# Two blocks on one core: merged rows made in columns, maxima before the gates' sums, compressed values made in columns, other places for the first query pieces

## The reference

```
blocks = t[:, :, tok] + pos
return blocks.reshape(B, G, n_cmp, CMP_LEN * dh) @ w
```

```
def merge(m, a, gates):
    g_m, g_a = jnp.split(gates, 2, axis=-1)
    return (jax.nn.sigmoid(g_m) * (m @ w_bm) + jax.nn.sigmoid(g_a) * (a @ w_ba)) @ w_out
```

## Time and profile before

| What | us |
|---|---|
| Median of the runs | 1293.1 |
| Profiled execution, its own time | 1294.55 |
| Span of that execution, first to last instruction | 1292.4 |
| TensorE busy with products | 1159.1 |
| VectorE busy | 860.6 |
| ScalarE busy | 313.9 |
| GpSimd busy | 326.1 |
| Mean granted TensorE clock, as a share of full speed | 0.981 |
| Memory traffic in all | 391.23 MB, mean 303 GB/s |

### The profile page before, as it was taken

The page is one execution under the profiler, slowest core; times in us unless marked ns, Lnnn a source line. Parts: engine busy times, 40 slices in busy tenths (PEclk is TensorE's granted clock), DMA queues, the critical chain, the costliest instruction groups (busy, mean ns, idle before and its releaser), DMA issues.

```text
span 1292.4 us, 14563 instructions
## 1 busy us (share of the span) xinstructions
PE 1159.1 (90%) x5048; PEld 695.6 (54%) x5048; DVE 860.6 (67%) x2306; ACT 313.9 (24%) x1008; POOL 326.1 (25%) x285
## 2 busy tenths in 40 slices
PE   8999999999999989999999889889877877778777
PEld 5876668867855677864566445445322322223332
DVE  2747745275545767873688777777778777777655
ACT  0115300234211122330232222222222222222222
POOL 0000000000001000000244454455554454554440
PEclk9999899999999999999999999999999899999999
DMA  8861155842343557632899999999999999999994
GB/s 340 308 253 66 65 195 210 301 156 99 125 195 134 213 160 267 244 130 98 318 405 424 424 424 424 425 424 424 423 424 422 424 424 424 423 421 424 423 424 200
DMA packets 54824, 391.23 MB, mean 303 GB/s; under 512 B 8120, under 2 KB 10680, under 8 KB 15840
## 3 DMA queue, kind: packets, MB, share of 16 engines
q0 software_dynamic: 37792, 269.63, 50.4%
q1 hardware_dynamic: 16960, 120.68, 24.9%
HBM read 389.22 MB, written 1.07 MB: 302 GB/s over the span
## 4 chain that ended last, share of the span: by engine, by line
PE 54%; DMA 34%; DVE 9%; ACT 2%; issue 1%; POOL 0%; SPq 0%; DVEq 0%; ACTq 0%
PE bank L541 20%; DMA wring<-peer_uv_in,arena 15%; PE bank L547 13%; PE bank L1124 10%; DMA const<-peer_uv_in,arena 7%; DMA arena<-peer_uv_in,arena 6%; DMA hT<-peer_uv_in,arena 5%; PE bank L576 2%; DVE arena L1601 1%; PE bank L769 1%; DVE arena L1609 1%; PE bank L613 1%; PE bank L599 1%; PE bank L683 1%; PE bank L741 1%
## 5 line engine op out<-in xcount | busy, mean ns | idle before, releaser
L1124 PE MATMUL bank<-arena 128*128 128x512 f32 x460 | 221.4, 618 | 44.0 <-ACT arena L1568 43.5
L1124 PE MATMUL bank<-wring,arena 128*128 128x512 f32 x340 | 164.2, 619 | 38.0 <-ACT arena L1568 38.0
L547 PE MATMUL bank<-hT,wring 128*128 128x256 f32 (+1 forms) x1088 | 188.9, 333 | 0.8 <-ACT arena L1346 0.8
L547 PEld LDWEIGHTS bank<-hT,wring 128*128 128x128 f32 x1088 | 169.2, 192 | 26.5 <-issue 11.2
L2317 DVE CUSTOM_DVE_ANT_0 arena<-arena 128x1024 f32<-128x1024 f32 x115 | 140.4, 1223 | 55.4 <-DMA arena<-peer_uv_in,arena 53.5
L1124 PEld LDWEIGHTS bank<-arena 128*128 128x128 f32 x460 | 85.8, 196 | 162.6 <-issue 93.0
L2422 POOL DMA_INDIRECT arena<-peer_uv_in,arena x114 | 131.8, 1156 | 162.5 <-PE bank L1124 136.3
L2387 POOL TENSOR_TENSOR small<-small,const 128x1 f32<-128x1 f32 (+3 forms) x18 | 16.7, 926 | 585.5 <-DVEq L1613 264.3
L541 PE MATMUL bank<-wring,hT 128*128 128x256 f32 (+2 forms) x544 | 157.9, 447 | 0.6 <-DVE arena L1601 0.6
L2317 DVE CUSTOM_DVE_ANT_0 wring<-wring,arena 128x1024 f32<-128x1024 f32 x85 | 103.9, 1223 | 44.1 <-DMA wring<-peer_uv_in,arena 43.2
L1124 PEld LDWEIGHTS bank<-wring,arena 128*128 128x128 f32 x340 | 63.2, 195 | 128.4 <-issue 65.5
(11 more groups left out here) (237 smaller groups left out, 1278.1 us busy)
## 6 DMA issues: line engine op xcount, KB each, us to landing
wring<-w_in SPq DMA_DIRECT2D x22, 2048.0 KB, 9.8
wring<-ada_in SPq DMA_DIRECT2D x12, 2048.0 KB, 8.4
wring<-wo_in SPq DMA_DIRECT2D x5, 2048.0 KB, 8.1
wring<-cmp_in SPq DMA_DIRECT2D x2, 2048.0 KB, 8.2
wring<-br_in SPq DMA_DIRECT2D x2, 2048.0 KB, 8.5
arena<-pq_in SPq DMA_DIRECT2D x2, 2048.0 KB, 9.4
wring<-pq_in SPq DMA_DIRECT2D x2, 2048.0 KB, 8.2
wring<-w1b_in SPq DMA_DIRECT2D x2, 1120.0 KB, 7.5
```

The lines of the kernel that those rows point to most:

```text
L547: ins = pe.matmul(bank[:, at:at + n_tok], w[:, k, col:col + P], rhs[:, k, :], start=(k == 0), stop=(k == KC - 1))
L1124: ins = pe.matmul(sums_of[half][:, :], diag[:, at % NDIAG, :], v_row[slot_of[at]][:, half * 512:(half + 1) * 512], start=(n == 0), stop=(n ...
```

## The change

**Compressed values.** The products get the keys' form: weights stationary, 15 columns moving, one bank `vcT` for both groups. ScalarE copies it to a corner of `cmp_s`, TensorE transposes it once behind the rotated queries and keys, and ScalarE copies the result to `vc` there.

**Maxima.** On VectorE `attn_max(0)` stands ahead of the running sums, `attn_scale(0)` behind them and ahead of the differences, `attn_max(1)` behind those, and the bias last.

**Merge.** `branch_gate` uses `project_t`, `branch` takes 16 products of 128 columns with the weights stationary, four side by side in a bank, and VectorE merges into `mrgT` directly, four blocks of 128. The transpositions of merged rows and their copies are gone; `out_rows` of half 0 waits for the first sum ahead of its first product and for the second ahead of the fifth.

**First rows.** The pieces of `plan` up to row 49 stand behind other rows, and the steps of heads 1 and 2 in `choice_at` too.

```
-        plan = [(row, ("q", 1, n, 0)) for n, row in enumerate((1, 1, 3, 3))] + [(5, ("ps", 0, 1)), (9, ("pT", 1))]
-        plan += [(row, ("q", 2, n, 0)) for n, row in enumerate((7, 11, 15, 19))] + [(21, ("ps", 0, 2))]
-        plan += [(row, ("q", 0, n, 1)) for n, row in enumerate((13, 17, 23, 25))]
-        plan += [(row, ("q", 3, n, 0)) for n, row in enumerate((31, 35, 39, 43))] + [(47, ("ps", 0, 3))]
+        plan = [(row, ("q", 1, n, 0)) for n, row in enumerate((1, 3, 5, 7))] + [(9, ("ps", 0, 1)), (11, ("pT", 1))]
+        plan += [(row, ("q", 2, n, 0)) for n, row in enumerate((13, 17, 21, 25))] + [(29, ("ps", 0, 2))]
+        plan += [(row, ("q", 0, n, 1)) for n, row in enumerate((15, 19, 23, 27))]
+        plan += [(row, ("q", 3, n, 0)) for n, row in enumerate((35, 39, 43, 47))] + [(49, ("ps", 0, 3))]
...
-            choice_at.setdefault(3 + n // 2, []).append((1, n))
+            choice_at.setdefault(3 + n * 5 // 16, []).append((1, n))
         for h in range(2, TT * EH):
-            first_row = 11 if h == 2 else 8 + 14 * (h - 2) if h < 6 else 16 * (h - 2)
+            first_row = 12 if h == 2 else 8 + 14 * (h - 2) if h < 6 else 16 * (h - 2)
             for n in range(16):
-                choice_at.setdefault(first_row + n * (11 if h == 2 else 14 if h < 6 else 16) // 16, []).append((h, n))
+                choice_at.setdefault(first_row + n * (10 if h == 2 else 14 if h < 6 else 16) // 16, []).append((h, n))
...
-                vc_bank = [job(("vc", L, g)) for g in range(2)]
+                bank = job(("vcT", L))
                 for l in range(CMP_L):
                     for g in range(2):
                         r = slice(g * HD, (g + 1) * HD)
-                        ins = pe.matmul(vc_bank[g][0:CMP_N, 0:HD], blocksT[r, 1, l, :], w[r, 1, l, :],
+                        ins = pe.matmul(bank[r, 0:CMP_N], w[r, 1, l, :], blocksT[r, 1, l, :],
                                         start=(l == 0), stop=(l == CMP_L - 1))
...
+                taken(pe, ("vcT", L))
+                bank = job(("vc", L))
+                finish(pe.transpose(bank[0:CMP_N, 0:P], vcT, ident), ("vc", L))
                 taken(pe, ("kc", L))
...
-                c, t, q = n // 4, (n // 2) % 2, n % 2
+                c, q = n // 4, n % 4
                 w = weights(("w2", 0, 6 + c)).rearrange("p (k c) -> p k c", k=KC)
-                project(("gate", n), [hlT[:, k, t * P:(t + 1) * P] for k in range(KC)], w[:, :, q * S:(q + 1) * S], S)
+                finish(project_t(job(("gate", n)), 0, w, q * P, hlT, S), ("gate", n))
...
-                project((name, half, t), [src[:, k, t * P:(t + 1) * P] for k in range(4)], wb[:, k0:k0 + 4, :], 512)
+                bank = job((name, half, t))
+                for q in range(4):
+                    for k in range(4):
+                        ins = pe.matmul(bank[:, q * P:(q + 1) * P], wb[:, k0 + k, q * P:(q + 1) * P], src[:, k, t * P:(t + 1) * P],
+                                        start=(k == 0), stop=(k == 3))
...
             def out_rows(half, t):
                 w = weights(("wo2", 0, half)).rearrange("p (k c) -> p k c", k=KC)
-                project(("wo2", half, t), [mrgT[:, k, t * P:(t + 1) * P] for k in range(KC)], w, 512)
+                bank = job(("wo2", half, t))
+                for k in range(KC):
+                    if half == 0 and k % 4 == 0:
+                        pe.wait_ge(sem("mrg"), 2 * t + k // 4 + 1)
+                    ins = pe.matmul(bank[:, :], mrgT[:, k, t * P:(t + 1) * P], w[:, k, :], start=(k == 0), stop=(k == KC - 1))
...
-            merged_transposes(0, 0)
             latent_transposes(1)
-            merged_transposes(0, 1)
...
-            merged_transposes(1, 0)
-            merged_transposes(1, 1)
             rows_back(0)
...
-            link(dve.memset(rows[7], 0.0))
...
             attn_max(0)
+            link(dve.memset(rows[7], 0.0))
...
+            attn_scale(0)
+            link(tt(rows[5], rows[0], rows[3], ALU.subtract))
+            link(tt(rows[6], rows[0], rows[4], ALU.subtract), "gate_rows")
             attn_max(1)
-            attn_scale(0)
+            add_bias(5, 6)
```

More of the change, by code:

```diff
@@ L1106, in _ @@
             head_scores(0)
-            merged_transposes(1, 0)
-            merged_transposes(1, 1)
             rows_back(0)
-            for half in range(2):
-                taken(pe, ("gT", 1, half))
             out_rows(0, 1)
@@ L1329, in _ @@
                     free(copy(retT[:, :, t * P:(t + 1) * P], bank[:, :].rearrange("p (j s) -> p j s", j=4)), ("rT", L, t))
+                bank = full(act, ("vc", L))
+                free(copy(vc[0:CMP_N, :], bank[0:CMP_N, 0:P]), ("vc", L))
                 for t in range(TT):
@@ L1500, in latent @@
                 free(copy(mT[:, :, t * P:(t + 1) * P], bank[:, :].rearrange("p (j s) -> p j s", j=4)), ("mT", t))
-            def merged(t):
-                for half in range(2 if t else 1):
-                    bank = full(act, ("gT", t, half))
-                    free(copy(mrgT[:, 4 * half:4 * half + 4, t * P:(t + 1) * P],
-                              bank[:, :].rearrange("p (j s) -> p j s", j=4)), ("gT", t, half))
             def x1_squares(t):
@@ L1544, in _ @@
             latent(0)
-            merged(0)
             latent(1)
```

53 lines of the change are left out of this document (22 added, 31 removed).

## The result

The changed kernel takes 1298.87 us (median of 6 runs, 1297.79 to 1300.24), the kernel before 1293.91 (6 runs): ratio 1.004, interval 1.0031 to 1.005. Slower by 0.4%, where 0.7% faster was forecast. The profiled execution has a span of 1296.0, 3.6 more than before.

A forecast was written before the change was run, and what follows sets the result against it. TensorE work, with VectorE pieces, bounds the kernel up to the first gather, expert-weight loads after it. 2.7 + 2.9 + 1.8 = 7.4, plus 0.5 and 1.0, gives 8.9 us off the median 1293.1: 1284.2, bounds 1281.5 to 1287.

The forecast's parts named there:

- Compressed values: Compressed stage of both layers: turned products save 1.47 less 0.13 for a transposition, 1.34 per layer, 2.7 us in all.
- Maxima: VectorE's order before the attention transpositions: TensorE's 2.86 us stop for scaled scores goes, worth 2.9 us, bounds 2.0 to 2.9.
- pause without a releaser: First layer's compressed stage: a pause that may go, counted only in the upper bound of 3.3 us.
- Gates, branches, merge: Before the first gather: gates nothing, merge saves 2.8, branches in columns lose 1.0; net 1.8 us, bounds 1.0 and 2.5.
- Behind the first gather: Second half of the kernel: 0.5 from earlier output projections and 1.0 from sparser first rows, 1.5 us together.
- gathers 2 to 8: First hole in the loads: their slots come 0.87 earlier without the merge's last transpositions; taken as 0.5 us, bounds 0 and 0.9.
- Head 1's indices: Selection on VectorE: done by row 7 instead of row 10, near 661, so gather 16 waits for its slot only.
- The second hole: Loads at 349 GB/s for 8 us from gather 16, 1.4 us lost; mostly goes, 1.0 us won, at worst 2 lost.
- (b): Rival: an early cut is taken up by a transfer or VectorE; 1287.1 if the maxima's 2.9 goes; chance 0.06.
- (d): Rival: the change doesn't do what it says, the transposed form's other waits cost what it saves: 1293; chance 0.03.

The follow-up runs named there:

- e8: The changed kernel with the gates' bias back in front of the maxima and compressed values in the old form: 1284.35 us, ratio 0.9944 to the kernel before.
- e1: The kernel before with the compressed values in columns alone: 1300.65 us, ratio 1.0057.
- e9: The changed kernel with the gates' bias early and every compressed key and value product moving 64 columns instead of 15: 1282.61 us, ratio 0.9921 to the kernel before.
- e13: The kernel before with only its compressed keys' products widened from 15 to 64 moving columns: 1290.34 us, ratio 0.9973.
- e5: The changed kernel with the bias of the gates' columns put back in front of the attention maxima: 1292.12 us, ratio 0.9995 to the kernel before.
- e14: The changed kernel, bias left late, with its thin compressed products widened to 64 moving columns: 1291.81 us, ratio 0.9984 to the kernel before.
- e2: The kernel before with the attention maxima in front of the gates' sums alone, the bias late: 1298.26 us, ratio 1.004.
- e11: The kernel before with the attention maxima first and the gates' bias kept early, nothing else: 1287.38 us, ratio 0.9955.
- e3: The kernel before with gates, branches and merge in columns alone: 1290.48 us, ratio 0.9973.
- e4: The kernel before with the sparser first rows and the denser selection alone: 1292.46 us, ratio 0.9994.
- e12: The changed kernel with bias early, compressed values in the old form and the row and selection tables of before: 1284.5 us, ratio 0.9933 to the kernel before.
- e6: The changed kernel with the compressed values' products in front of the keys': 1300.92 us, ratio 1.0063 to the kernel before.
- e10: The changed kernel, bias early, compressed keys and values both in the old form with 64 moving columns, keys then transposed: 1281.05 us, ratio 0.9914 to the kernel before.

## Why the prediction was wrong

**Compressed values: the step failed.** I took -1.34 per layer from two neighbouring rows, 5.31 us for the old form and 3.84 for the turned one, as the prices of two forms. They were taken at two clocks. At the full clock the old form takes 3.75 (e8) and the turned one 3.91, so the change had nothing to gain there but what the fall of the clock had cost. The one price that it did have stood in none of my terms: around the end of the keys' 15-column products the clock falls, and the turned form puts a second run of them there. They ran at the lower level, and so did part of the dense product behind them: +2.9 and +3.3 in the trace, 7 us for the step alone (e1). The two rows had a different granted clock, 1.00 and 0.68; the windows of that stretch would have shown it before any argument about forms. I also had the hint of a "pause without a releaser" in layer 0 and took its end for a possible gain; pauses of 0.43 and 0.36 us stand in e9 and e13 too, at a clock of 1.00, so they are not the fall.

By the rule of the Trainium skill (TensorE: Matmul & The Clock Gate, LDWEIGHTS) I had estimated 6.8 us for the turned form, and the trace now says 6.9. That is not the rule coming true: at the full clock the same 128 loads of 64 columns, with their products, take 3.8 to 4.1 us (3.91 for the keys in this trace, 3.95 in e9). The same page of the Trainium skill, in its section HAM oscillation — how this bites in real kernels, tells of a kernel with thin matmuls that falls back to the lower clock, in its case through waits for transfers. The trace shows the lower clock here without any wait for a transfer, behind the thin products themselves. So that part would not have forecast this loss as it stands, but it was the one about the clock, and I weighed the other one.

**Maxima: the gain was right, what is queued behind it was missed.** The stop of 2.86 went (-2.95) and with it 1.7 of lower clock that I could have read from the timeline of the kernel before: 8.75 for the second half against 7.17 for the first. The failed sentence is "SP waits for the gates' rows only together with a transposition that TensorE makes after its second half". It is true of the semaphore `gate_rows`. But SyncE's block waits for the bias as well, a few lines above, and the change puts the bias behind the second round of maxima. I had costed its end (462.1; it came at 469.2, which is 462.9 less the shift of 6.3) and not followed who waits for it: SyncE, a transfer of 10.9 us for 4 KB, and a heap of loads behind it. That was +6.4 in the trace, and 6 to 11 us between kernels with and without it (e5, e14, and e2 against e11).

**Gates, branches, merge: right.** 1.8 forecast, 1.8 in the trace; 3.4 us with what it frees (e3).

**Behind the first gather: right in kind, a little small.** 1.5 forecast, 2.6 found, of which gathers 2 to 8 have 1.1 (0.5 forecast). Head 1's indices came in time: no gather behind the first waits for VectorE any more, and gather 16 leaves 37.75 us behind the first instead of 42.44. The second hole is gone from the trace (426 GB/s from 676.2 to 684.2, where 349 had been). But the gathers then wait for slots on TensorE's side, and the hole's filling shows in no median (e4, e12).

**The rivals.** None of mine had this result's cause. (b), the shift lost on its way to a transfer, was near the second one, but I argued it away with "the chain has no transfer there", reading the chain of the kernel before, in which that transfer had 7 us of cover (it landed around 465 and SyncE asked for it at 472). (d) put the loss in the turned form's waits, and the place was right, the mechanism not. My sum without the compressed values' term, 1286.9, less the 1.7 of clock that I hadn't counted, is 1285.2; e8 has 1285.9 by its ratio. The arithmetic of the rest held, the 1.1 us more behind the first gather aside.

## What to carry to other kernels

Before the ratio of two rows is taken as the ratio of two forms, read the granted clock of both stretches; a row at a mean clock between the levels is a price of neither. Here a run of products that move few columns was dearer than its own row shows, since the clock fell behind it for what follows; widening the products over columns that nobody reads cost next to nothing (3.95 us for 3.91) and won 9.6 us in e9, though in e13 only half of the executions gained clearly. And when an instruction is moved back on its engine, follow each semaphore that it raises through every queue: the cover of a small transfer is as much a resource as a slot.

## What the runs showed of the hardware

- 64 products on 64 rows (128 records) take 3.75 to 4.07 us at the full clock, with weights of 64 columns and 15 moved (3.91 to 3.94), 64 and 64 (3.94 to 4.07) or 15 and 64 (3.75 to 4.04); with 15 moved at the lower clock they take 6.99 to 7.07.
- Two runs of them with 15 columns moved, one behind the other: in all eight such stretches of the profiled executions (two layers each of the changed kernel, e1, e5 and e6) the clock fell, in the second half of the first run or early in the second, with no wait for another engine or a transfer; the dense product behind took 8.75 to 10.10 us. With the first run widened to 64 columns it stayed at 1.00 in all eight (e9, e10, e13, e14).
- With thin keys and wide values, the form of before, it fell in eight of fourteen stretches and not in the other six, with the same code there: the values took 5.38 us in one and 3.75 in another. In all fourteen the dense product behind took 7.13. What decides between the two is not shown.
- A transfer of 4 KB from 128 partitions into a row took 10.9 us to land in the changed kernel while the load engines moved next to nothing (medians of two such transfers 10.7 to 14.7 in all traces), longer than the median of 2 MB loads there (7.6 to 9.7 for those that are issued more than once).
